# Two fused transformer blocks on one core: a third tile joins the block-interleaved opening after a norm, and the second sum moves behind it

## The chip, the cores and the metric

One core of one Trainium2 chip runs the whole program. The metric is the device time of one launch in microseconds (us); less is better.

## What is computed

A sequence of 512 tokens of width 1024 goes through a first block (an RWKV-7 mix and dilated attention, cross attention to a memory of 256 tokens, a squared-ReLU feed-forward) and then through a second block of two layers (a Fourier mix and a chunked retention, then a feed-forward with a width-3 convolution over tokens), with a normalisation ahead of each part. What matters here is the form that recurs at each part's border:

```
h = h + gate * (y @ w_last)                     # residual, [512 tokens, 1024]
n = h * rsqrt(mean(h*h, over 1024) + 1e-6) * g  # norm: one number per token
n = n * (1 + scale) + shift                     # second block only
z = n @ w_next                                  # the next stage's matmuls
```

The norm needs the sum over all 1024 features of a token before the first product of the next stage can start for that token.

## The kernel before, in words

Activations lie with the features on the partitions: 8 blocks of 128 features, each 512 tokens wide (`KT` = 8, `S` = 512). A matmul stage is a row of *tiles*: an output tile is 128 output features by 512 tokens in one of four PSUM banks, and sums 8 (or 6) blocks `k`. Each float32 product is made of three fp32r matmuls (L670 weights high x activation high, L671 weights high x activation low, L672 weights low x activation high).

Weights arrive in *units* of 128x1024 in a ring of four (`RING`): SyncE loads `w_raw`, ScalarE (ACT) casts it to `w_hi` (L1356), GpSimd (POOL) makes `w_lo` by four subtractions (L613), and TensorE (PE) waits for `w_low`. In the stages touched here a tile of 8 blocks has a unit of its own. ACT may cast a unit only when PE has ended the tile that used its slot four units earlier.

**Norms by token half.** At six places the norm is split into two halves of 256 tokens (`W2`). The names of the norms are `ffn` (closed by the stage `x_out`, followed by `up0`), `final` (closed by `down3`, followed by `fourier_in0`), `n2_0` and `n2_1` (closed by `out0`, `out1`, followed by `ff_in0_0`, `ff_in1_0`), `n1_1` (closed by `ff_out0_2`, followed by `fourier_in1`) and `out` (nothing follows). In the *closing* stage the last four tiles (`TAIL`) are made half by half. Then:

- VectorE (DVE) adds a tile half into the residual `H` (L1984 without a gate, L1985 with one), ACT squares it (L1416), DVE adds the squares up (L1938).
- PE sums over the partitions with four small products, `both_sums` (L706 for the running sum, L710 for the last square; at `final` a second pair L722, L726).
- DVE makes the statistic (L1919; four small operations at `final`), POOL raises it to -1/2 (L627), PE spreads it over the partitions into a bank (`spread_half`, L789).
- DVE multiplies block j of H by it into `tmp` (L2039), ACT makes the high part (L1376), DVE the low part (L1900, or L1898 at `ffn`). PE may use block j of that half once its low part is there.

The order of the DVE in `split_halves` is written by hand: blocks i = 0 to 7 are of the first token half, 8 to 15 of the second. Ahead of i = 1, 3, 5 it also takes the remaining tiles' second halves (`LATE_AT`), ahead of i = 6 it makes the statistic of the second half (`STAT_AT`), and there it waits for PE's sum of that half. The low part of block i-1 always follows the `tmp` of block i. The spread of the second half is waited for ahead of i = 8.

The *opening* of the next stage is `opening_halves` on PE: its first three tiles t0, t0+1, t0+2 are made half by half. The first half goes block by block over the first two tiles, and PE's sum of the second half stands behind block 2, its spread behind block 6. Then comes the whole first half of t0+2, then the second half of the first two tiles block by block, then the second half of t0+2. After the opening, the next tiles are made whole (512 tokens).

ACT's part in the closing is `closing` at L1421: squares and casts. `spare_slots(name)` says how many units of the next stage have a free slot before the last closing tile has ended: 1 for `n1_1` (its closing stage has tiles of 6 blocks, so the last units hold more than a tile), and 0 for all the others. POOL's program makes the low part of that spare unit ahead of the first half's L627 (`half_requests`), in the order in which the requests stand.

Of the kernel before, what the change touches and what calls it, by code (L numbers as in the profile page):

```python
# [25 lines left out]
KT = D // P  # L26
# [197 lines left out]
def build_program(nc, plan, ap, out):  # L224

    tiles, stages, conv, splits = plan.tiles, plan.stages, plan.conv, plan.splits
# [8 lines left out]
    for u in sorted(last_block):  # L235
        t, i = last_block[u]
# [7 lines left out]
    with ctx:  # L244
# [5 lines left out]
        def sem(name):  # L250
            if name not in sems:
                sems[name] = ctx.enter_context(nc.semaphore(name))
            return sems[name]
# [161 lines left out]
        def evacuated(eng, t):  # L415

            eng.wait_ge(sem(f"bank_free{bank_of(t)}"), tiles[t]["use"])
# [132 lines left out]
        def spare_slots(name):  # L550

            t0, t1 = stages[CLOSED[name]][0] + FULL, stages[CLOSED[name]][1] - 1
            return RING - 1 - tiles[t1]["blocks"][-1][0] + tiles[t0]["blocks"][0][0]
# [78 lines left out]
        def _(pe):  # L632
# [81 lines left out]
            def both_sums(norm, h):  # L714

                sum_half(norm, h)
                if norm == "final":
                    s = FULL + TAIL * h + TAIL - 1
                    chunks = range(TC // 2 * h, TC // 2 * (h + 1))
                    pe.wait_ge(sem("scaled_sq_used"), s)  # L720
                    for c in chunks:
                        nc.tensor.matmul(banks[5][:, TC + c:TC + c + 1], scaled_square_sum[:, c * P:(c + 1) * P],  # L722
                                         ones[:, 0:1], start=(c == chunks[0]), stop=False, skip_group_check=True)
                    pe.wait_ge(sem("scaled_sq_ready"), s + 1)
                    for c in chunks:
                        mm = nc.tensor.matmul(banks[5][:, TC + c:TC + c + 1], scaled_squares[:, s % 2, c * P:(c + 1) * P],  # L726
                                              ones[:, 0:1], start=False, stop=True, skip_group_check=True)
                    mm.then_inc(sem("scaled_sq_used"), 1)

            def spread_half(norm, h):  # L730

                if norm == "final":
                    pe.wait_ge(sem("both_inverses"), h + 1)
                spread(banks[7 if h else 4], W2, first=TC // 2 if norm == "final" else 0)
# [16 lines left out]
                for t in (t1 - 2, t1 - 1):  # L751
                    tile(t, splits[split][0], half=1, norm=norm)

            def opening_halves(name, split, norm):

                t0 = stages[name][0]
                for k in range(KT):
                    for t in (t0, t0 + 1):
                        tile(t, splits[split][0], only=k, half=0)
                    if k == 2:  # L760
                        both_sums(norm, 1)
                    if k == KT - 2:
                        spread_half(norm, 1)
                tile(t0 + 2, splits[split][0], half=0)
                for k in range(KT):
                    for t in (t0, t0 + 1):
                        tile(t, splits[split][0], only=k, half=1)
                tile(t0 + 2, splits[split][0], half=1)

            def spread_residual():  # L770

# [176 lines left out]
            t0 = stages["rkv1"][0]  # L948
# [134 lines left out]
            t0, t1 = stages["attn_out"]  # L1083
# [91 lines left out]
            for c, _ in enumerate(chunks_of(FF1)):  # L1175
                for name, split in ((f"up{c}", "n_ffn"), (f"down{c}", f"hidden{c}")):
                    t0, t1 = stages[name]
# [25 lines left out]
            for l in range(LAYERS):  # L1203
                t0 = stages[f"fourier_in{l}"][0]
# [13 lines left out]
                def fourier_tokens(j):  # L1218
# [16 lines left out]
                    mm.then_inc(sem("f_made"), 1)  # L1235

                opening_halves(f"fourier_in{l}", f"n1_{l}", f"n1_{l}" if l else "final")
                if l == 0:
                    spread_residual()
# [90 lines left out]
        def _(act):  # L1330
# [55 lines left out]
            def cast_opening(name, count):  # L1386

                if count:
                    cast_to(max(u for t in range(stages[name][0], stages[name][0] + count) for u, _, _ in tiles[t]["blocks"]))
# [31 lines left out]
            def closing(name, following=None):  # L1421

                t0 = stages[CLOSED[name]][0]
                for j in range(FULL):
                    follow(t0 + j)
                    evacuated(act, t0 + j)
                    square(name, j, H[:, j, :])
                    if name == "final":
                        scaled_square(j, j, slice(0, S))
                follow(t0 + FULL)  # L1430
                for j in range(FULL, KT):
                    square_half(name, j, 0)
                    cast_to(tiles[t0 + KT - 1]["blocks"][-1][0])
                if following:
                    cast_opening(following, spare_slots(name))
                square_half(name, FULL, 1)
                if following:
                    cast_opening(following, 1)
# [264 lines left out]
            t0, t1 = stages["mem_v"]  # L1703
# [32 lines left out]
            t0 = stages["x_out"][0]  # L1736
# [4 lines left out]
            for c, _ in enumerate(chunks_of(FF1)):  # L1741
                q = splits[f"hidden{c}"][0]
                t0, t1 = stages[f"up{c}"]
# [17 lines left out]
            for l in range(LAYERS):  # L1761
# [6 lines left out]
                t0 = stages[f"fourier_in{l}"][0]  # L1768
# [75 lines left out]
                for c, (a, n) in enumerate(chunks_of(FF2)):  # L1844
                    t0 = stages[f"ff_in{l}_{c}"][0]
# [13 lines left out]
                    t0 = stages[f"ff_out{l}_{c}"][0]  # L1859
# [872 lines left out]
```

## Time and profile before

| | |
|---|---|
| median of the 3 runs | 3442.48 us (3441.59 to 3443.18) |
| the profiled execution's own time | 3446.2 us |
| its span, first to last instruction | 3444.4 us |
| PE busy | 3358.8 us (98%) |
| DVE, ACT, POOL busy | 1573.0, 1124.5, 1567.3 us |
| mean granted TensorE clock | 0.994 of full |

PE is busy nearly all the time, so a change of order can only win or lose in the short stretches where it waits, and in the stretches where its granted clock is below 1. A busy PE in the table says little, as each matmul's recorded 0.28 us overlaps the next one, which starts 0.12 us later. The distance between two starts is the measure to use.

### The profile page before, as it was taken

To read this page: it belongs to the slowest core of one execution; us is meant where nothing else is said; L and a number is where in the kernel's file an instruction comes from. 1 tells how busy PE (TensorE), PEld (TensorE's weight loads), DVE (VectorE), ACT (ScalarE), POOL (GpSimd) and SP (SyncE) were. 2 spreads that over 40 slices of the span, in tenths; PEclk is the share of its full clock that TensorE was granted. 3 is DMA by queue.
4 is the path that set the end of the run, shared out by engine and by line. 5 is a ranking of instruction groups with operands and counts; after the bars stand their busy time and mean duration, and the time that the engine had idled before them with its cause. 6 is when DMAs were issued, how large, how long until landed. Compare 5 with 4: busy or idle time off the path is not lost.

```text
span 3444.4 us, 46412 instructions
## 1 busy us (share of the span) xinstructions
PE 3358.8 (98%) x17992; PEld 2821.8 (82%) x17992; DVE 1573.0 (46%) x2347; ACT 1124.5 (33%) x1780; POOL 1567.3 (46%) x1932
## 2 busy tenths in 40 slices
PE   7989999999999999999999999999999999999998
PEld 6768888888887888888887878888888787788887
DVE  2347766675232376666312214734551222255435
ACT  3333333333224332224322223423332222243323
POOL 4312111221456376764353345656534443556555
PEclk9999999999999999999999999999999999999999
DMA  4201000011333156672232223233222322223232
GB/s 151 68 25 39 25 25 25 25 48 36 125 95 120 62 208 238 239 255 80 74 105 78 67 85 98 86 98 105 87 71 86 97 73 79 86 86 106 91 98 92
DMA packets 91834, 321.70 MB, mean 93 GB/s; under 512 B 9952, under 2 KB 14176, under 8 KB 91360
## 3 DMA queue, kind: packets, MB, share of 16 engines
q1 hardware_dynamic: 83936, 299.93, 26.9%
q10 hardware_dynamic: 7680, 18.80, 1.6%
q8 instruction: 144, 2.36, 0.3%
q14 instruction: 74, 0.61, 0.1%
HBM read 314.76 MB, written 3.93 MB: 93 GB/s over the span
## 4 chain that ended last, share of the span: by engine, by line
PE 68%; POOL 13%; issue 12%; DVE 5%; DMA 1%; ACT 1%; POOLq 0%; DVEq 0%; SPq 0%; ACTq 0%
PE bank L670 16%; PE bank L672 15%; PE bank L671 15%; POOL w_lo L613 12%; PE bank L905 5%; PE bank L911 2%; PE bank L1277 1%; PE bank L663 1%; PE bank L665 1%; PE bank L664 1%; DMA w_raw<-in_weights 1%; PE bank L1214 1%; PE bank L1290 1%; DVE act L1900 1%; PE bank L846 1%
## 5 line engine op out<-in xcount | busy, mean ns | idle before, releaser
L613 POOL TENSOR_TENSOR w_lo<-w_raw,w_hi 128x256 fp32r<-128x256 f32 x1888 | 1520.8, 838 | 1248.4 <-ACT w_hi L1356 1248.2
L670 PE MATMUL bank<-act,w_hi 128*128 128x512 f32 (+1 forms) x3776 | 1440.5, 381 | 16.4 <-POOL w_lo L613 9.4
L672 PE MATMUL bank<-act,w_lo 128*128 128x512 f32 (+1 forms) x3776 | 1406.7, 373 | 0.0
L671 PE MATMUL bank<-act,w_hi 128*128 128x512 f32 (+1 forms) x3776 | 1406.1, 372 | 0.0
L670 PEld LDWEIGHTS bank<-act,w_hi 128*128 128x128 f32 x3776 | 716.3, 190 | 150.9 <-issue 31.0
L672 PEld LDWEIGHTS bank<-act,w_lo 128*128 128x128 f32 x3776 | 715.4, 189 | 123.6
L671 PEld LDWEIGHTS bank<-act,w_hi 128*128 128x128 f32 x3776 | 716.6, 190 | 120.1 <-issue 5.7
L1356 ACT CAST w_hi<-w_raw 128x1024 fp32r<-128x1024 f32 x472 | 489.3, 1046 | 393.1 <-PE bank L672 182.2
L627 POOL TENSOR_TENSOR stats<-stats,exponent 128x8 f32<-128x8 f32 (+2 forms) x39 | 46.9, 1204 | 627.8 <-DVE stats L1919 436.7
L1364 ACT ACTIVATE arena<-bank 128x512 f32<-128x512 f32 (+2 forms) x203 | 117.6, 585 | 511.5 <-PE bank L672 504.0
L905 PE MATMUL bank<-arena 128*128 128x128 f32 (+1 forms) x1920 | 247.1, 276 | 3.5 <-DVE arena L2269 2.5
L905 PEld LDWEIGHTS bank<-arena 128*128 128x128 f32 x1920 | 231.3, 192 | 16.3 <-issue 6.6
L1898 DVE TENSOR_TENSOR act<-tmp,act 128x512 fp32r<-128x512 f32 (+1 forms) x172 | 145.8, 848 | 84.5 <-ACT act L1376 78.2
L1376 ACT CAST act<-tmp 128x512 fp32r<-128x512 f32 (+1 forms) x172 | 100.2, 586 | 178.8 <-DVE tmp L2513 48.2
L1589 ACT ACTIVATE arena<-bank 128x512 f32<-128x512 f32 x144 | 85.1, 597 | 155.3 <-PE bank L911 155.0
L2583 DVE TENSOR_SCALAR arena<-arena,params 128x512 f32<-128x512 f32 x88 | 51.3, 583 | 178.1 <-ACT arena L1364 177.8
L2378 DVE TENSOR_TENSOR arena<-arena,bank 128x512 f32<-128x512 f32 x32 | 22.0, 687 | 235.9 <-PE bank L672 235.9
L2447 DVE SCALAR_TENSOR_TENSOR arena<-arena,small 128x1024 f32<-128x1024 f32 x84 | 122.0, 1453 | 3.0
L2056 DVE SCALAR_TENSOR_TENSOR arena<-bank,small,arena 128x512 f32<-128x512 f32 x48 | 36.0, 751 | 169.2 <-PE bank L672 169.0
L911 PE MATMUL bank<-table,arena 128*128 128x128 f32 x640 | 97.0, 276 | 13.1 <-DVE arena L2269 8.9
L663 PE MATMUL bank<-w_hi,act 128*128 128x256 f32 (+2 forms) x352 | 108.4, 308 | 1.3 <-POOL w_lo L613 1.3
L664 PE MATMUL bank<-w_lo,act 128*128 128x256 f32 (+2 forms) x352 | 106.7, 303 | 0.0
(251 smaller groups left out, 3054.7 us busy)
## 6 DMA issues: line engine op xcount, KB each, us to landing
w_raw<-in_weights SPq DMA_DIRECT2D x472, 512.0 KB, 3.5
arena<-in_ada SPq DMA_DIRECT2D x96, 512.0 KB, 4.4
arena<-in_strips ACTq DMA_DIRECT2D x8, 448.0 KB, 4.4
arena<-in_x ACTq DMA_DIRECT2D x4, 512.0 KB, 8.0
arena<-in_x ACTq DMA_DIRECT2D x1, 2048.0 KB, 8.0
y_scratch<-tmp ACTq DMA_DIRECT2D x7, 256.0 KB, 2.7
arena<-y_scratch ACTq DMA_DIRECT2D x1, 1792.0 KB, 9.1
arena<-in_dft ACTq DMA_DIRECT2D x2, 896.0 KB, 4.6
```

The source lines that it names most:

```text
L613: ins = nc.gpsimd.tensor_tensor(w_lo[:, k, cols], w_raw[:, k, cols], w_hi[:, k, cols].bitcast(F32), ALU.subtract)
L663: nc.tensor.matmul(o, xs[0], wh, start=first, stop=False)
L664: nc.tensor.matmul(o, xs[0], wl, start=False, stop=False)
L670: nc.tensor.matmul(o, wh, xh, start=first, stop=False)
L671: nc.tensor.matmul(o, wh, xl, start=False, stop=False)
L672: mm = nc.tensor.matmul(o, wl, xh, start=False, stop=last)
L905: mm = nc.tensor.matmul(b[:, w * i:w * (i + 1)], lhs[:, c, :], rhs(c), start=True, stop=True)
L911: mm = nc.tensor.transpose(b[:, P * i:P * (i + 1)], src[:, 4 * h + i, :], ident)
L1356: nc.scalar.copy(w_hi[:, k, :], w_raw[:, k, :]).then_inc(sem("w_high"), 1)
L1364: nc.scalar.activation(dst, banks[bank_of(t)][:, 0:n], func, scale=scale).then_inc(sem(f"bank_free{bank_of(t)}"), 1)
L1898: do(V_.tensor_tensor(o, x, h, ALU.subtract), "low_done")
L2447: do(V_.scalar_tensor_tensor(o, w, c_act[:, k:k + 1], o, ALU.mult, ALU.add), "ada_used")
```

## The change

Three things move; nothing is added to or taken out of any engine's work.

1. On PE, in `opening_halves`: in the first token half, tile t0+2 runs beside the first two from block 4 of these on, four blocks behind (`lag`), rather than behind them. In the second token half all three tiles go block by block.
2. On PE: the sum of the second half stands behind block 4 (and behind the third tile's block 0), no longer behind block 2. The spread stays behind block 6, but three blocks of the third tile now stand ahead of it.
3. On ACT, in `closing`: the spare unit of the next stage is cast after the first of the four half squares, no longer after the last. As `spare_slots` is 0 elsewhere, this moves one instruction, at `n1_1`.

```diff
-            def opening_halves(name, split, norm):
+            def opening_halves(name, split, norm, lag=4):
 
                 t0 = stages[name][0]
+                for k in range(KT + lag):
+                    if k < KT:
+                        for t in (t0, t0 + 1):
+                            tile(t, splits[split][0], only=k, half=0)
+                    if k >= lag:
+                        tile(t0 + 2, splits[split][0], only=k - lag, half=0)
+                    if k == 4:
+                        both_sums(norm, 1)
+                    if k == 6:
+                        spread_half(norm, 1)
                 for k in range(KT):
-                    for t in (t0, t0 + 1):
-                        tile(t, splits[split][0], only=k, half=0)
-                    if k == 2:
-                        both_sums(norm, 1)
-                    if k == KT - 2:
-                        spread_half(norm, 1)
-                tile(t0 + 2, splits[split][0], half=0)
-                for k in range(KT):
-                    for t in (t0, t0 + 1):
+                    for t in range(t0, t0 + 3):
                         tile(t, splits[split][0], only=k, half=1)
-                tile(t0 + 2, splits[split][0], half=1)
...
                 for j in range(FULL, KT):
                     square_half(name, j, 0)
                     cast_to(tiles[t0 + KT - 1]["blocks"][-1][0])
-                if following:
-                    cast_opening(following, spare_slots(name))
+                    if following:
+                        cast_opening(following, spare_slots(name))
                 square_half(name, FULL, 1)
```

How the instructions stand. PE at the opening of `ff_in0_0` (norm `n2_0`; its tiles t0, t0+1, t0+2 are in bank2, bank3, bank0), around the sum of the second half. Before, behind block 2 of t0+1:

```order
L672 MATMUL bank3<-act1,w_lo 128x256
L706 MATMUL bank5<-table,square_sum 128x1 x2
L710 MATMUL bank5<-table,squares 128x1 x2
L670 MATMUL bank2<-act1,w_hi 128x256
L671 MATMUL bank2<-act1,w_hi 128x256
```

With the change, behind block 4 of t0+1 and block 0 of the third tile (bank0):

```order
L672 MATMUL bank3<-act1,w_lo 128x256
L670 MATMUL bank0<-act1,w_hi 128x256
L671 MATMUL bank0<-act1,w_hi 128x256
L672 MATMUL bank0<-act1,w_lo 128x256
L706 MATMUL bank5<-table,square_sum 128x1 x2
L710 MATMUL bank5<-table,squares 128x1 x2
L670 MATMUL bank2<-act1,w_hi 128x256
```

The row behind L710 was block 3 of t0; it is now block 5 of t0. The other openings read alike.

ACT in the closing of `n1_1`. Before, the cast of the spare unit is the second L1356 here:

```order
L1356 CAST w_hi<-w_raw 128x1024
L1416 ACTIVATE squares<-arena 128x256 x4
L1356 CAST w_hi<-w_raw 128x1024
L1416 ACTIVATE squares<-arena 128x256
L1762 DMA arena<-in_dft 128x1792
```

With the change (the same lines, one number up):

```order
L1357 CAST w_hi<-w_raw 128x1024
L1417 ACTIVATE squares<-arena 128x256
L1357 CAST w_hi<-w_raw 128x1024
L1417 ACTIVATE squares<-arena 128x256 x4
L1763 DMA arena<-in_dft 128x1792
```

The cast passed three of the half squares. DVE, POOL and SyncE keep their order.

## Rows read from the trace of the kernel before

**Rows 1.** The page, part 1: busy time of each engine.
```profile
PE 3358.8 (98%) x17992; PEld 2821.8 (82%) x17992; DVE 1573.0 (46%) x2347; ACT 1124.5 (33%) x1780; POOL 1567.3 (46%) x1932
```

**Rows 2.** Waits of PE, 1190 to 3100 us: total us, times, longest.
```profile
PE bank L706 <- DVE square_sum L1938: 3.9, 4, 1.4
PE bank L710 <- ACT squares L1416: 2.2, 4, 1.2
```

**Rows 3.** Timeline of PE, n2_0: start, us, what, [idle before <-releaser].
```profile
2148.57 0.28 PE L672 MATMUL bank<-act,w_lo 128*128 128x256 f32 x1
2149.72 0.61 PE L706 MATMUL bank<-table,square_sum 128*128 128x1 f32 x4 [0.88 <-DVE square_sum L1938]
2150.69 0.61 PE L710 MATMUL bank<-table,squares 128*128 128x1 f32 x4 [0.36 <-ACT squares L1416]
```

**Rows 4.** Timeline of DVE, n2_0: low parts 3, 4; statistic; low part 5.
```profile
2148.32 0.48 DVE L1900 SCALAR_TENSOR_TENSOR act<-tmp,small,act 128x256 fp32r<-128x256 f32 x1
...
2150.22 0.48 DVE L1900 SCALAR_TENSOR_TENSOR act<-tmp,small,act 128x256 fp32r<-128x256 f32 x1
...
2151.39 0.16 DVE L1919 TENSOR_SCALAR stats<-bank 128x2 f32<-128x2 f32 x1 [0.17 <-PE bank L710]
...
2152.11 0.48 DVE L1900 SCALAR_TENSOR_TENSOR act<-tmp,small,act 128x256 fp32r<-128x256 f32 x1
```

**Rows 5.** Timelines, norm ffn: PE's sum without a wait, DVE's statistic.
```profile
1212.85 0.50 PE L706 MATMUL bank<-table,square_sum 128*128 128x1 f32 x4
...
1213.74 0.37 PE L670 MATMUL bank<-act,w_hi 128*128 128x256 f32 x1
...
1213.97 0.16 DVE L1919 TENSOR_SCALAR stats<-bank 128x2 f32<-128x2 f32 x1 [0.23 <-PE bank L710]
```

**Rows 6.** PE in windows: from:to us, busy (count), granted clock, DMA share, GB/s.
```profile
1211.00:1216.00 5.00, 5.00 (x43) 1.00 0.92 334
...
2152.80:2155.80 3.00, 3.00 (x16) 0.50 0.00 0
```

**Rows 7.** Timeline of PE, norm final: the waits ahead of the two sums.
```profile
1596.41 0.61 PE L706 MATMUL bank<-table,square_sum 128*128 128x1 f32 x4 [0.78 <-DVE square_sum L1938]
1598.17 0.61 PE L710 MATMUL bank<-table,squares 128*128 128x1 f32 x4 [1.16 <-ACT squares L1416]
```

**Rows 8.** Timelines at n2_0: PE's first whole tile, ACT's cast of t0+5.
```profile
2168.69 0.40 PE L670 MATMUL bank<-act,w_hi 128*128 128x512 f32 x1
2168.92 0.40 PE L671 MATMUL bank<-act,w_hi 128*128 128x512 f32 x1
...
2172.95 1.05 ACT L1356 CAST w_hi<-w_raw 128x1024 fp32r<-128x1024 f32 x1 [1.34 <-DVE arena L2586]
```

**Rows 9.** Page, part 5: the group of POOL's subtractions.
```profile
L613 POOL TENSOR_TENSOR w_lo<-w_raw,w_hi 128x256 fp32r<-128x256 f32 x1888 | 1520.8, 838 | 1248.4 <-ACT w_hi L1356 1248.2
```

**Rows 10.** Timelines at n1_1: ACT takes t0, DVE's fold, PE's use.
```profile
2536.06 1.08 ACT L1364 ACTIVATE arena<-bank 128x512 f32<-128x512 f32 x2
...
2538.92 0.71 DVE L2504 TENSOR_TENSOR arena<-arena 128x128 f32<-128x128 f32 x1
...
2540.85 1.46 PE L1214 MATMUL bank<-arena 128*128 128x256 f32 x6
```

**Rows 11.** Timelines behind norm final: DVE's fold, PE's use of it.
```profile
1621.08 0.29 DVE L2504 TENSOR_TENSOR arena<-arena 128x128 f32<-128x128 f32 x1
...
1621.51 0.67 PE L1214 MATMUL bank<-arena 128*128 128x256 f32 x2 [0.16 <-DVE arena L2504]
```

**Rows 12.** Timelines, n1_1, first half: ACT's cast, DVE's statistic, POOL, PE's spread.
```profile
2504.97 1.03 ACT L1356 CAST w_hi<-w_raw 128x1024 fp32r<-128x1024 f32 x1
...
2507.06 0.16 DVE L1919 TENSOR_SCALAR stats<-bank 128x2 f32<-128x2 f32 x1 [2.45 <-PE bank L710]
...
2508.83 0.70 POOL L627 TENSOR_TENSOR stats<-stats,exponent 128x2 f32<-128x2 f32 x1
...
2509.59 0.71 PE L789 MATMUL bank<-table,stats 128*128 128x128 f32 x4 [1.08 <-POOL stats L627]
```

## The prediction, made before the changed kernel ran

> **What bounds the kernel now.** I read the page's busy times first: PE is busy for 98% of the span [rows 1], so what this change of order can win or lose lies where PE waits or runs at a lower clock. Next the waits of PE over the stretch that holds the five openings: 3.9 us ahead of L706, 2.2 us ahead of L710 [rows 2], and once 1.1 us ahead of L789 [rows 12]. All lie in the norms. Then the timelines. At `n2_0`, block 2 of t0+1 has its last start at 2148.57, then PE sits until 2149.72 for DVE's running sum, and again ahead of L710 for ACT's last square [rows 3]. At `final` the same two waits are 0.78 and 1.16 us [rows 7]. At `ffn` there is neither [rows 5]. Last the granted clock in windows: behind the `n2_0` waits it is 0.50, the 1.2 GHz level, and PE starts 16 matmuls in 3.00 us; at clock 1.00 there are 43 in 5.00 us [rows 6]. The same lower stretch follows the waits at `final`, `n1_1` and `n2_1`, with 15 or 16 matmuls in 3.00 us each; at `ffn` there is none. What PE did before each fall was to wait and to make one-column sums.
>
> From these rows: a matmul of 256 tokens starts 0.12 us after the last (5.00 / 43), so a block of one tile is 0.36 us and a block of three tiles 1.08 us. At the lower clock the step is 0.19 to 0.21 us, so a lower stretch costs about 16 x 0.09 = 1.5 us where PE has work all through it. A sum that waits for nothing is 0.89 us (1212.85 to 1213.74), and the statistic starts 1.12 us after the sum does [rows 5].
>
> **The sum behind block 4, at n2_0.** Up to block 2 nothing changes: PE is through at 2148.57 + 0.12 = 2148.69. Block 3 needs low part 3, ready at 2148.80, so it runs 2148.84 to 2149.56. Block 4 needs low part 4, which DVE ends at 2150.22 + 0.48 = 2150.70 [rows 4]. So PE waits here for 1.2 us, about what the sum waited. The wait at the sum is gone but is not saved. Blocks 4, 4 and the third tile's 0 end at 2151.90, the sum at 2152.79, and the statistic starts at 2151.90 + 1.12 = 2153.02, where it was 2151.39.
>
> Here a new wait arises. DVE stands at its statistic, and queued behind it are tmp 6 and then low part 5, in this order. Low part 5 ends 2152.59 - 2151.39 = 1.20 us after the statistic starts [rows 4], now at 2154.22. PE's next instruction is block 5 of t0, which needs it. Before, blocks 3 and 4 of two tiles (4 x 0.36 = 1.44 us) stood between the sum and block 5, and covered this chain. Now nothing does: **PE waits 2154.26 - 2152.79 = 1.4 us.** The third tile's block 1 would fit there, but it stands behind block 5.
>
> From there: blocks 5 and 6 with the third tile's (2 x 1.08, and 0.08 for a first matmul after a wait) end at 2156.50, the spread takes 0.36, seven blocks 2.52, and the 24 blocks of the second half 8.64 and about 0.1. The opening ends at 2168.1. It ended at 2168.69 [rows 8], 1.3 us of that by the lower clock, so 2167.4 at a full one. The order alone is worth +0.7 us: two waits of 2.6 us for 1.6 us before, less about 0.3 us at blocks of the second half, which three tiles per block (1.08 us) give DVE time to make. The same steps with the rows of the other openings give +0.8 at `ffn` (no wait before, 1.4 us after), +0.6 at `final` (a wait of 2.0 us for low part 4, 2.2 us for low part 5, as there two pairs of sums and four statistics stand in the chain), +0.6 at `n1_1` and `n2_1`. Sum: **+3.2 us**.
>
> **The clock.** The sum and its waits at `n2_0` left PE without wide matmuls for 2.5 us (2148.69 to 2151.16), and the clock fell. Now 1.2 + 0.9 + 1.4 = 3.5 us are without them, with 1.16 us of work between. I expect the fall at the four places again, about 0.2 us dearer each at three, since more work stands behind; at `final`, where 5.9 us are without work, a longer one (+1.0 us); and a new one at `ffn` (+1.4), where 0.9 + 1.4 us are. Sum: **+2.8 us**. Both ends: 0 if the clock falls as before, and minus 4 x 1.5 = -6 if it no longer falls at all; +6 if it stays low for a second stretch at four places.
>
> **What follows the opening.** Tile t0 ended about 3.2 us before the opening's end (the eight blocks of t0+2, and one of t0+1); now it ends 0.72 us before it. ACT casts the unit of t0+4 on t0's end and only then takes t0 out of its bank, so this chain comes 2.6 us later against PE. (a) At `n1_1` DVE's fold of t0 ended at 2539.63, 3.57 us after ACT's take began, and PE used it at 2540.85 [rows 10]: 1.2 us of cover. It will be 2.6 us later, less the cover: **+1.6 us** with what the wait takes to end. (b) Behind `final`, the fold waits for a residual spread that stays in place, but POOL's subtractions of t0+4 now lie on it. A fold operation of 128 columns takes 0.29 us without POOL [rows 11] and 0.71 us beside it [rows 10]; the wait there is already on PE's path: **+0.9 us**. (c) At `n2_0` and `n2_1` the cast of t0+5 hangs on DVE's second convolution, 4.3 us after the opening's end [rows 8]. At 6.9, and with 1.1 for the cast and 3.4 for POOL's part (4 x 838 ns [rows 9]), the unit is ready 11.4 us after. PE needs it two tiles after, at 11.0 (24 matmuls of 512 tokens at 0.23 us each [rows 8]): **+1.0 us** for both. At `ffn` 0.1 to 1 us of cover remains. The three sum to 3.5 us; bounds 0 (DVE and ACT catch up) and 7 (each late by the whole 2.6).
>
> The SBUF — State Buffer page of the Trainium skill ("SBUF: two separate sides") says that a DVE operation with two SBUF inputs and a GpSimd operation that reads SBUF exclude each other for a whole instruction. By that, each of the four fold operations could lose up to a whole subtraction of POOL, and (b) would be near 3 us by the page's rule. The trace agrees in kind, 0.29 to 0.71 us [rows 10, 11], and the sum uses the rows.
>
> **The cast.** At `n1_1` ACT cast the spare unit at 2504.97, POOL's low part of it ran until 2508.83, and only then came L627, though the statistic had been there since 2507.22; PE waited until 2509.59 [rows 12]. Cast some 6 us sooner, POOL is free, L627 ends near 2508.0, and PE, ready at 2508.35, does not wait: **-1.2 us**. The cast holds up nothing: the next half square comes 1 us after it would end. Its bounds are -1.3 and 0 (if the slot is not free then, but the tile that used it ends before it).
>
> **Sum:** 3.2 + 2.8 + 3.5 - 1.2 = +8.3 us. Against the profiled execution's 3446.2 us that is 3454.5; the median of the runs lies 3.7 us lower, 3442.5, so I predict **3450.8 us**. A measurement of this kernel can tell about 0.2%, 6.9 us, from no change.
>
> **The rivals.** *The new wait, with clock and followers as forecast*: 3450.8, chance 0.55. *The order alone*: the clock falls as before and ACT and DVE catch up, so 3.2 - 1.2 = +2 us, to +6 with half of the followers: 3444 to 3449, chance 0.24. For it speaks that both followers have some cover, which the rows show only to 1 us. *Clock low twice*: a second lower stretch at three or four places, and units late for PE: +13 to +16 us, 3455 to 3459, chance 0.14. *Faster*: DVE's low part 5 is not the limit. PE would lose its waits of 3.9 + 2.2 us [rows 2], four lower stretches of 1.5 us and the 1.2 us of the cast: -13 us, 3429. It decides at block 5: low part 5 must be ready when the sum ends. Its chain hangs on that very sum, by 1.45 us at least, so only a mistake in the order I read would give it; chance 0.04. *Only the cast works*, all the rest even: -1 us, 3441, chance 0.03.
>
> **The range** takes in 3444 to 3458: it leaves out the two cases at the fast side, and the far end of the slow one. The chances: faster by over 0.2% is the fourth case, 0.04. Slower by over 0.2% is above 3449.4: three quarters of the first case, whose middle lies 1.4 us above that bound, and all of the third, 0.41 + 0.14 = 0.55. The rest, 0.41, lies within.
>
> **What would show it.** In the profile of the changed kernel: at each of the five openings a wait of PE at block 5 (L670 for DVE's L1900 or L1898) of 1.4 us, 2.2 at `final`, and one at block 4 at four of them; waits of L706 and L710 gone; statistic 1.6 us later against the closing stage; a lower clock also behind `ffn`; a wait of about 1.6 us for L2504 at `fourier_in1`; no wait at L789 (L790 there) at `n1_1`. It is wrong if low part 5 is there before the sum ends, or if the lower stretches go.

## The result, and the profile after

The changed kernel takes 3458.04 us (median of 4 runs, 3456.72 to 3459.87). The kernel before, run beside it, takes 3442.69 us (4 runs, 3441.59 to 3443.18). The ratio is 1.004, with a 95% interval of 1.0028 to 1.0052: slower, by 15.4 us, where +8.3 us was forecast. A second measurement, with 5 runs against 15, gave 3460.15 against 3444.03 us: 1.0047 (1.0034 to 1.0061); one of the 15 was a slow run of 6827 us, which the ratio leaves out. The profiled execution of the changed kernel took 3456.72 us (span 3454.9, mean granted clock 0.994), that of the second measurement 3459.49 us (span 3457.7, clock 0.993).

The page of the changed kernel, part 1, busy time of each engine:

```profile
PE 3356.0 (97%) x17992; PEld 2818.5 (82%) x17992; DVE 1579.8 (46%) x2347; ACT 1124.5 (33%) x1780; POOL 1573.7 (46%) x1932
```

The instructions are as many as before [rows 1]; DVE and POOL are each busy for 6 to 7 us more. The time is lost where PE waits and where its clock is low. Its waits from 1190 to 3110 us (total us, times, longest):

```profile
PE bank L670 <- DVE act L1901: 11.2, 9, 2.1
PE bank L670 <- POOL w_lo L613: 9.2, 9, 3.5
...
PE bank L670 <- DVE act L1899: 1.3, 1, 1.3
PE bank L1215 <- issue: 1.2, 1, 1.2
PE bank L1215 <- DVE arena L2505: 0.9, 1, 0.9
```

The two rows of before, 3.9 us at L706 and 2.2 us at L710 [rows 2], are gone. In their place stand 12.5 us at L670 for DVE's low parts. At `n2_0`, PE's timeline of the changed kernel reads:

```profile
2156.77 0.38 PE L670 MATMUL bank<-act,w_hi 128*128 128x256 f32 x1 [0.94 <-DVE act L1901]
2157.95 0.50 PE L706 MATMUL bank<-table,square_sum 128*128 128x1 f32 x4
2158.31 0.58 PE L710 MATMUL bank<-table,squares 128*128 128x1 f32 x4
2160.24 0.43 PE L670 MATMUL bank<-act,w_hi 128*128 128x256 f32 x1 [1.35 <-DVE act L1901]
```

The first wait is at block 4, the two sums run without one, and the last wait is at block 5. Against before [rows 3], two waits of 1.24 us in all have become two of 2.29 us. The chain of waits of the changed kernel shows what the second is made of (start, us, what):

```profile
2158.45 0.46 PE bank L710 x4
2158.91 0.03 DVEq L1916
...
2158.99 0.17 DVE stats L1920
2159.18 0.49 DVE tmp L2040
...
2159.70 0.50 DVE act L1901
...
2160.24 0.43 PE bank L670
```

So it is as forecast: the end of the sum releases DVE's statistic, DVE then makes `tmp` 6 and only behind it low part 5, and PE has nothing else to do. The low part is there 1.21 us after the statistic starts, as before (1.20 us) [rows 4]. The statistic itself starts 13.39 us after the spread of the first half (2158.99 - 2145.60), where it was 11.79 us: 1.6 us later, as forecast.

**Where the clock fell.** Windows of PE (from:to us, busy and count, granted clock, DMA share, GB/s), each around one place (`down0` is the stage behind `up0`; its first tile comes some 30 us behind the opening at `ffn`). First the changed kernel: `down0`, `final`, `n2_0`, `n1_1`, `n2_1`:

```profile
1255.00:1270.00 15.00, 11.45 (x41) 0.77 0.64 216
1595.00:1615.00 20.00, 15.80 (x112) 0.83 0.32 102
2148.00:2168.00 20.00, 17.70 (x133) 0.91 0.34 105
2510.00:2540.00 30.00, 27.09 (x202) 0.89 0.36 119
3065.00:3095.00 30.00, 27.71 (x229) 1.00 0.23 71
```

The changed kernel in the second measurement, `ffn` and then the same places from `down0` on:

```profile
1210.00:1225.00 15.00, 13.71 (x103) 0.89 0.43 171
1255.00:1270.00 15.00, 11.46 (x51) 1.00 0.71 244
1595.00:1615.00 20.00, 15.80 (x98) 0.74 0.28 81
2148.00:2168.00 20.00, 17.70 (x133) 0.91 0.33 105
2510.00:2540.00 30.00, 27.12 (x201) 0.89 0.39 119
3065.00:3095.00 30.00, 27.71 (x209) 0.89 0.22 71
```

The kernel before, `n2_0` and `n2_1` (at `final` it reads 0.91, at `n1_1` 0.94):

```profile
2148.00:2168.00 20.00, 18.70 (x141) 0.91 0.21 74
...
3065.00:3095.00 30.00, 28.71 (x196) 0.94 0.24 72
```

A window of 20 us at 0.91 holds 3.6 us at half clock (0.09 x 2 x 20). Counted so over the five openings, PE had 14.4 us at the 1.2 GHz level before, 17.0 us in the changed kernel's first profile and 30.5 us in its second, and the first has 6.9 us more at `down0`. PE's waits for DVE were the same in both profiles (12.5 and 12.4 us), and the one at `down0` too (3.5 us); where the clock fell differs.

**Against the stretches.** The same matmul was found in two traces and its two starts subtracted; what the difference gains over a stretch is what the stretch cost. "Opening" is up to the first whole tile, "behind" is the next tile or two (for `ffn`, up to `down0`'s first tile). In us, against the trace before, which is one and the same execution for all columns and lay 3.7 us above its median, so that a column reads some us lower than the medians do:

| stretch | change | change, second | sum back | old second half | statistic later | filled | filled, ffn as before | take first |
|---|---|---|---|---|---|---|---|---|
| up to `ffn` | -1.5 | -2.1 | -2.6 | -1.7 | -0.6 | -1.2 | -0.7 | -1.7 |
| opening `ffn` | +0.9 | +2.4 | -0.5 | +3.3 | -0.2 | -0.1 | 0 | 0 |
| behind `ffn` | +4.4 | +1.9 | +3.5 | 0 | +3.5 | +3.2 | 0 | 0 |
| opening `final` | +1.7 | +3.3 | -0.9 | +4.5 | +0.7 | -1.3 | -0.6 | -0.6 |
| behind `final` | +0.8 | +0.8 | +0.8 | 0 | +0.8 | +0.8 | +0.8 | +1.0 |
| opening `n2_0` | +0.9 | +1.0 | -1.9 | +2.4 | -1.6 | -2.6 | -2.6 | -2.6 |
| behind `n2_0` | +1.2 | +1.2 | +1.2 | 0 | +1.2 | +1.2 | +1.2 | +0.3 |
| closing of `n1_1` | -1.4 | -1.3 | -1.3 | -1.4 | -1.3 | -1.3 | -1.4 | -1.3 |
| opening `n1_1` | +1.9 | +2.1 | -0.3 | +3.1 | -0.5 | -2.6 | -2.5 | -2.6 |
| behind `n1_1` | +1.5 | +1.5 | +1.5 | 0 | +1.5 | +1.5 | +1.5 | 0 |
| opening `n2_1` | -0.5 | +2.0 | -1.8 | +3.1 | -1.5 | -2.5 | -2.6 | -2.5 |
| behind `n2_1` | +0.9 | +0.9 | +0.9 | 0 | +0.9 | +0.9 | +0.9 | +0.3 |
| the whole span | +10.5 | +13.3 | -1.7 | +13.5 | +2.4 | -4.1 | -6.0 | -9.7 |

The columns behind the first two are experiments, in the order of the sections below. Stretches that are not listed differ by 0.5 us or less in all. Ahead of `ffn` the change moves nothing; that row goes with the clock from 1000 to 1190 us, which was 0.97 of full in the trace before, 0.99 in the change's first profile and 1.00 in its second.

**Behind `ffn`** is the largest single row, and the forecast had nothing there. PE's first tile of `down0`, in the trace of before and in that of the change:

```profile
1259.55 0.47 PE L670 MATMUL bank<-act,w_hi 128*128 128x512 f32 x1 [1.66 <-POOL w_lo L613]
```

```profile
1260.85 0.76 PE L670 MATMUL bank<-act,w_hi 128*128 128x512 f32 x1 [3.55 <-POOL w_lo L613]
```

POOL's timeline of the 32 us ahead of it, before:

```profile
1227.96 8.31 POOL L613 TENSOR_TENSOR w_lo<-w_raw,w_hi 128x256 fp32r<-128x256 f32 x8 [7.86 <-ACT w_hi L1356]
1237.62 4.70 POOL L613 TENSOR_TENSOR w_lo<-w_raw,w_hi 128x256 fp32r<-128x256 f32 x4 [1.35 <-ACT w_hi L1356]
1243.06 9.92 POOL L613 TENSOR_TENSOR w_lo<-w_raw,w_hi 128x256 fp32r<-128x256 f32 x8 [0.74 <-ACT w_hi L1356]
1253.94 5.46 POOL L613 TENSOR_TENSOR w_lo<-w_raw,w_hi 128x256 fp32r<-128x256 f32 x4 [0.96 <-ACT w_hi L1356]
```

and with the change:

```profile
1229.90 36.83 POOL L613 TENSOR_TENSOR w_lo<-w_raw,w_hi 128x256 fp32r<-128x256 f32 x30 [9.50 <-ACT w_hi L1357]
```

POOL starts the unit of t0+4 late, because that unit's cast waits for tile t0, which now ends late: 0.66 us behind the end of the opening (1229.90 against 1229.24), where it was 1.86 us ahead of it (1227.96 against 1229.82), so 2.5 us later against PE. Before, POOL had three gaps (1.35 + 0.74 + 0.96 = 3.05 us), and PE waited even then. The three are gone now, which would take the lateness in, but the 24 subtractions ahead of `down0`'s first tile take 30.8 us in place of 28.4. In this stretch a subtraction takes 0.73 us where no DVE operation is under way at its start, and about 1.18 or 1.72 us where one is; five of the 24 were of the short kind before, one is with the change. So 1.9 of the 2.5 us reach PE.

**The fold and the cast** came as forecast. Behind `final` and at `n1_1` the changed kernel's PE shows a wait in front of L1215:

```profile
1627.52 0.67 PE L1215 MATMUL bank<-arena 128*128 128x256 f32 x2 [0.95 <-DVE arena L2505]
...
2550.87 1.32 PE L1215 MATMUL bank<-arena 128*128 128x256 f32 x5 [1.22 <-issue]
```

It was 0.16 us and nothing [rows 10, 11]. The second one is put down to "issue", but it ends with DVE's fold: its last operation ran from 2550.07 for 0.70 us. ACT's order decides it too, as an experiment below shows. And the spread of the first half at `n1_1`, one line up from L789, waits for nothing, where PE waited 1.08 us [rows 12]; POOL's subtractions end at 2512.13, 3 us ahead of the statistic:

```profile
2507.31 4.82 POOL L613 TENSOR_TENSOR w_lo<-w_raw,w_hi 128x256 fp32r<-128x256 f32 x6
2515.39 0.69 POOL L627 TENSOR_TENSOR stats<-stats,exponent 128x2 f32<-128x2 f32 x1 [3.27 <-DVE stats L1920]
2516.43 0.60 PE L790 MATMUL bank<-table,stats 128*128 128x128 f32 x4
```

### The profile page after: what moved, and what is told of

It reads as the page before. It is cut to its first block, busy times and chain, and to the rows that moved or that the text cites. A ratio compares the mean times of both kernels' runs of the same rounds, so it can differ in the third digit from the quotient of the medians.

```text
span 3454.9 us, 46412 instructions
## 1 busy us (share of the span) xinstructions
PE 3356.0 (97%) x17992; PEld 2818.5 (82%) x17992; DVE 1579.8 (46%) x2347; ACT 1124.5 (33%) x1780; POOL 1573.7 (46%) x1932
## 3 DMA queue, kind: packets, MB, share of 16 engines
q8 instruction: 144, 2.36, 0.3%
## 4 chain that ended last, share of the span: by engine, by line
PE 71%; POOL 11%; issue 11%; DVE 5%; ACT 1%; DMA 1%; POOLq 0%; DVEq 0%; SPq 0%; ACTq 0%
PE bank L670 17%; PE bank L672 16%; PE bank L671 16%; POOL w_lo L613 11%; PE bank L906 5%; PE bank L912 2%; PE bank L1278 1%; PE bank L663 1%; PE bank L665 1%; PE bank L664 1%; PE bank L1215 1%; PE bank L1291 1%; PE bank L847 1%; PE bank L790 1%; PE bank L876 1%
## 5 line engine op out<-in xcount | busy, mean ns | idle before, releaser
L670 PE MATMUL bank<-act,w_hi 128*128 128x512 f32 (+1 forms) x3776 | 1441.2, 382 | 32.9 <-POOL w_lo L613 13.6
L670 PEld LDWEIGHTS bank<-act,w_hi 128*128 128x128 f32 x3776 | 716.5, 190 | 169.1 <-issue 36.1
L663 PE MATMUL bank<-w_hi,act 128*128 128x256 f32 (+2 forms) x352 | 108.0, 307 | 2.9 <-POOL w_lo L613 2.9
L665 PE MATMUL bank<-w_hi,act 128*128 128x256 f32 (+2 forms) x352 | 106.5, 302 | 0.0
```

Of the source, the lines that this page charges most:

```text
L663: nc.tensor.matmul(o, xs[0], wh, start=first, stop=False)
L665: mm = nc.tensor.matmul(o, xs[1], wh, start=False, stop=last)
L670: nc.tensor.matmul(o, wh, xh, start=first, stop=False)
```

## The experiments

### The cast alone

The kernel before, with the third part of the change only:

```diff
                     cast_to(tiles[t0 + KT - 1]["blocks"][-1][0])
-                if following:
-                    cast_opening(following, spare_slots(name))
+                    if following:
+                        cast_opening(following, spare_slots(name))
```

> The kernel before with the cast of n1_1's spare unit after the first half square, and nothing else. The theory (POOL is late for the statistic of n1_1's first half only because it still makes the spare unit's low part): PE's wait of 1.1 us at L789 goes, nothing else moves, 1.2 us less than before, 3441.5. The rival (the earlier subtractions hold up DVE's adds in the closing stage, which then end later): no gain, 3442.7, with the sum of the first half later than before against the closing tiles.

Measured: 3442.49 us against 3443.34, ratio 0.9999 (0.999 to 1.0008). The wait in front of the spread is gone and the closing of `n1_1` is 1.35 us shorter, in this trace as in all the others with the cast. A gain of 0.04% does not show in the medians, which cannot tell 3441.5 from the rival's 3442.7; the trace does.

This trace tells something else too. It differs from the one before in a single instruction's place, and yet its span is 5.1 us shorter: besides the cast's 1.35 us, 1.9 us ahead of `ffn`, 0.9 at the opening of `n2_0` and 0.8 at that of `n2_1`. At the last two its clock did not fall:

```profile
2148.00:2168.00 20.00, 19.50 (x147) 1.00 0.18 55
...
3065.00:3095.00 30.00, 29.49 (x191) 1.00 0.24 71
```

At `final` and `n1_1` it fell as before. So a fall at a given opening is no fixed thing, and the profiled execution of before, 3.7 us above its median, was one with more of them. The kernel before shows the same with nothing moved: its executions in the second measurement run from 3441.26 us at a mean granted clock of 0.997 to 3449.31 us at 0.992. The forecast took its four falls for the rule.

### The second sum back behind block 2

The change, with the third tile where it puts it, but the sum in its old place:

```diff
-                    if k == 4:
+                    if k == 2:
                         both_sums(norm, 1)
```

> The change with the sum of the second half behind block 2 again (the third tile still four blocks behind, the second half by three tiles, the early cast). First theory (the sum behind block 4 makes the wait at block 5): the waits of PE for low part 5 (1.3 us at four openings, 2.1 us at final) go, the old waits at L706 and L710 come back (about 6 us in all), and what follows the openings stays as late as in the change: 6 us less than the change, 3452. Rival (the place of the sum does not matter, the order of the second half does): as the change within 1 us, 3457 to 3459.

Measured: 3445.72 us against 3443.34, ratio 1.0009 (1.0000 to 1.0018): 12 us below the change, twice what was expected. The waits in front of L706 and L710 are back (3.9 and 2.2 us), the followers are what they are with the change, and the openings cost 10.3 us less. So the sum's place is the costly part. In this trace it is dearer than the waits it makes (12.5 us in place of 6.1), since at `n2_0` and `n2_1` the clock did not fall (1.00 in both windows) and at `final` and `n1_1` it fell for half as long.

### The second half in its old order

The change, with t0 and t0+1 first and then t0+2 in the second token half:

```diff
-                    for t in range(t0, t0 + 3):
+                    for t in (t0, t0 + 1):
                         tile(t, splits[split][0], only=k, half=1)
+                tile(t0 + 2, splits[split][0], half=1)
```

> The change with its second half as before: two tiles block by block, then the third. First theory (what follows an opening is late because t0 ends only 0.7 us before the opening's end): the long wait for w_lo at down0's first tile falls from 3.5 us back to about 1.8 us, the fold at fourier_in1 is in time, and the waits at block 5 stay. The openings end 1.2 us later each (low part 14 sets the end), so the whole is about 2 us less than the change, 3456. Rival (the order of the second half is all that costs): as the kernel before within 2 us, 3441 to 3445.

Measured: 3457.69 us against 3443.34, ratio 1.0041 (1.0028 to 1.0054), the same as the change, where 3456 was expected. All the followers are gone (0 in all five rows of the table), which shows that the late end of t0, which the three-tile second half brings, caused every one of them. The openings pay it back. This trace has the clock falls of the change's second profile, and its openings cost 16.4 us where those cost 10.8. PE's timeline at `n2_0` shows why; here are the first matmuls of three successive blocks of t0 in the second half:

```profile
2168.72 0.39 PE L670 MATMUL bank<-act,w_hi 128*128 128x256 f32 x1
...
2169.76 0.39 PE L670 MATMUL bank<-act,w_hi 128*128 128x256 f32 x1
...
2170.80 0.39 PE L670 MATMUL bank<-act,w_hi 128*128 128x256 f32 x1
```

Two tiles per block are 0.72 us of work, and they come 1.04 us apart: DVE makes a low part in 1.04 us, and PE loses 0.3 us at each block, in pieces too short for the table of waits. Three tiles per block take 1.08 us and lose nothing. At `n2_0` the old order costs 1.4 us here (2.36 against 0.95). The kernel before lost only some 0.3 us in this way, as the forecast had it, since there the whole first half of t0+2 stood ahead of the second half and gave DVE a lead.

### The statistic one block later on DVE

The change, with DVE's statistic of the second half ahead of i = 7. Low part 5 then no longer stands behind it:

```diff
-        LATE_AT, STAT_AT, CAST_AT = (1, 3, 5), 6, (0, 2, KT - 1)
+        LATE_AT, STAT_AT, CAST_AT = (1, 3, 5), 7, (0, 2, KT - 1)
```

> The change with one number altered: DVE makes the second half's statistic ahead of its block 7, no longer ahead of block 6. PE's order is that of the change. First theory (the wait at block 5 is the chain statistic, tmp 6, low part 5 behind the sum): low part 5 is ready before the sum ends, the waits of 1.3 us at block 5 fall to nothing, one of about 0.3 us appears at block 6 (1 us at final), and the lower clock is rarer; about 1 us less at each opening, 6 us less than the change in all, 3451 to 3453. Rival (PE waits at block 5 since ACT and DVE are simply that slow per block): the waits keep their length, 3457.

Measured: 3447.10 us against 3442.88, ratio 1.0011 (1.0003 to 1.0020): 11 us below the change, nearly twice what was expected. PE at `n2_0`, ahead of the sum and at block 5:

```profile
2155.81 0.50 PE L706 MATMUL bank<-table,square_sum 128*128 128x1 f32 x4
...
2158.10 0.38 PE L670 MATMUL bank<-act,w_hi 128*128 128x256 f32 x1 [0.17 <-DVE act L1901]
```

The block-5 wait has shrunk from 1.35 to 0.17 us, by one instruction moved on an engine that is busy for 46% of the span. The clock at `n2_0` and `n2_1` stayed at 1.00. This is the cleanest proof that the wait is DVE's order behind the late sum: nothing on PE moved. The wait at block 4 is as in the change (0.93 us), and the kernel stays slower than the one before.

### The waits filled from the third tile

Blocks of t0+2 are at hand, so PE can do them where it would wait. The first half as a row of steps, where a digit is a block of t0 and t0+1, a letter a block of t0+2 (a is 0), S the sum and P the spread:

```diff
-                for k in range(KT + lag):
...
+                for step in ("0123abcS4def56g7Ph" if norm == "final" else "0123abcS4de5Pf67gh"):
```

The second half is as in the change, and the cast too.

> A first half in another order: blocks 0 to 3 of the two tiles, the third tile's 0 to 2, the sum, block 4, the third tile's 3 and 4, block 5 and so on (at final one block more between sum and block 5), with the second half and the cast of the change. First theory (what costs is that PE has nothing in its order between the sum and low part 5): no wait of PE over 0.3 us from block 3 to block 7 except at final (1 us for ACT's last square), no lower clock behind four of the five openings, openings that end 3 us sooner than before at four places and even at ffn; the followers stay as late as in the change (8 us in all). About 6.5 us less than before, 3436. Rival (the clock falls wherever the one-column sums stand, whatever is around them): the lower stretches stay at four places, 3441 to 3443.

Measured: 3443.41 us against 3443.34, ratio 0.9999 (0.999 to 1.0008). The openings gain: they are 9.1 us shorter than before. But the followers are there, with 7.6 us, 3.2 of them behind `ffn`. Expected was 3436, with 8 us of followers counted in. What fell short is the gain at the openings (3 us at four places expected, 2.5 to 2.6 measured at three and 1.3 at `final`) and the base: the span is 4.1 us shorter than that of the trace before, the median the same, as the execution in that trace was a long one.

With the old second half besides:

```diff
-                    for t in range(t0, t0 + 3):
+                    for t in (t0, t0 + 1):
                         tile(t, splits[split][0], only=k, half=1)
+                tile(t0 + 2, splits[split][0], half=1)
```

> The filled first half with the second half of the kernel before (two tiles block by block, then the third) and the early cast. First theory (DVE makes a block per 1.04 us in the second half and PE takes 0.72 us for two tiles, so the opening ends 4.3 us after low part 14, and the followers are in time): openings end about 1.9 us later than in the filled order, no wait for w_lo over 1.9 us at down0, none over 0.3 us at the folds; within 1 us of the filled order, 3442.5. Rival (the three-tile second half wins nothing): 8 us less than the filled order, 3435.

Measured: 3443.01 us against 3442.88, ratio 0.9999 (0.999 to 1.0008). No followers now, and the openings are back to -0.4 us in all. Both forms end where the kernel before does: the three-tile second half is worth 8.7 us at the openings here and costs 7.6 behind them.

### The opening at ffn left alone

There no wait could be won [rows 5], and the follower is dearest:

```diff
+                order = {"final": "0123abcS4def56g7Ph", "ffn": "012S3456P7abcdefgh"}
...
+                    for t in range(t0, t0 + (2 if norm == "ffn" else 3)):
...
+                if norm == "ffn":
+                    tile(t0 + 2, splits[split][0], half=1)
```

> The filled order of the last experiment, with norm ffn's opening wholly as in the kernel before. First theory (the late wait at down0's first tile comes from ffn's opening alone: t0 ends 1.9 us later there, and POOL's subtractions then run without a gap up to down0): the wait for w_lo at down0 is 1.8 us again, no lower clock follows it, and 3 to 4.4 us are won over the filled order, all ahead of 1262 us: 3438 to 3440. Rival (that wait has another cause, such as how the transfers fall): it stays at 3.5 us and the time stays at 3443.4.

Measured: 3439.73 us against 3442.88, ratio 0.9986 (0.9977 to 0.9995). Its repeat:

> The filled order with ffn as before once more, on the same chip as e8: as it was, 3 us less than before.

Measured: 3439.63 against 3443.44 us, ratio 0.9988 (0.9979 to 0.9997). The interval stays below 1 in both: faster, by 3 to 4 us. Windows of the first of the two at `n2_0`, `n1_1` and `n2_1`:

```profile
2148.00:2168.00 20.00, 19.75 (x153) 1.00 0.21 68
2510.00:2540.00 30.00, 27.93 (x202) 1.00 0.21 71
3065.00:3095.00 30.00, 29.13 (x189) 1.00 0.23 64
```

### ACT takes t0 before it casts for t0+4

What is left are the followers behind four openings, 4.4 us. ACT hangs both on t0's end: first the cast of t0+4's unit, then the taking of t0 out of its bank, on which DVE's fold or convolution waits. Exchanged, at the four openings other than `ffn` (the second piece stands behind the activation that takes a tile out of its bank):

```diff
-                cast_opening(following, 5)
+                if norm == "ffn":
+                    cast_opening(following, 5)
+                else:
+                    pending.append(following)
...
+                if pending:
+                    cast_opening(pending.pop(), 5)
```

> The filled order with ffn as before, and ACT takes t0 out of its bank before it casts the unit of t0+4, at the four openings other than ffn's. Theory for what follows an opening (ACT's cast of 1.05 us stands ahead of the take, and DVE's fold or convolution behind it): the fold at fourier_in1 is about 1 us sooner, so PE's wait there falls from 1.5 us to under 0.5, the waits behind n2_0 and n2_1 (1.2 and 0.9 us) fall to 0.2 or less, the one behind final stays at 0.8, as it hangs on the residual spread; 3 us less than the filled order with ffn as before, 3437. Rival (POOL's subtractions beside DVE set these waits, not ACT's order): they stay as they are or grow, since the cast is later, 3440 or more.

Measured: 3436.49 us against 3443.44, ratio 0.9977 (0.9968 to 0.9986). Its timeline at `n1_1`, ACT and then PE:

```profile
2530.12 0.60 ACT L1369 ACTIVATE arena<-bank 128x512 f32<-128x512 f32 x1 [2.04 <-PE bank L672]
2530.61 1.04 ACT L1361 CAST w_hi<-w_raw 128x1024 fp32r<-128x1024 f32 x1
...
2533.34 1.89 PE L1218 MATMUL bank<-arena 128*128 128x256 f32 x8
```

The take runs first and PE finds the fold done: the wait of 1.2 us is gone. The followers at `n2_0`, `n1_1` and `n2_1` fall from 3.6 to 0.6 us. The one behind `final` stays (+1.0): PE waits there for the first fold however ACT is ordered.

> The filled order with ffn as before and the early take, once more, beside the change on the same chip: 7 us under before, 0.9968 to 0.9986 again, and some 20 us under the change.

Measured: 3437.57 against 3444.03 us, ratio 0.9978 (0.9969 to 0.9987). This version beats the kernel before by 6.5 to 7 us, the changed one by about 22.

### The change once more

> The change itself once more, beside the kernel before on one chip. The profiled executions differ by 10.5 us and the medians by 15.4. If the rest is where the granted clock falls from one execution to the next (the profiled one fell in three of the five openings and stayed up at ffn and n2_1), this profile shows it fall at ffn or n2_1 too, with 1 to 2 us more in the stretch concerned and the same waits to 0.1 us. If it is something else, a stretch outside the openings and what follows them differs from the first profile by over 1 us with the clock at full. Time 12 to 15 us over before.

Measured: 3460.15 us (3459.49 to 3460.75) against 3444.03, as told at the top. Its waits for DVE are those of the first profile (11.1 us in place of 11.2 for L1901), its clock is not: it fell at `ffn` and at `n2_1` too, and these openings cost 1.5 and 2.5 us more. The time is 16.1 us over before, where 12 to 15 were expected.

## Why the prediction was right, and where it was short

The sign and the mechanism held; the size, +8.3 us forecast and +15.4 measured, did not. The 3458.04 us lie at the very end of the range, and among the times of the third rival, "Clock low twice" (3455 to 3459, chance 0.14), not near the 3450.8 of the first. The sum has slips too, which change little: its terms for the order add up to 3.3 us and not 3.2, those for the clock to 3.0 and not 2.8, and 2154.26 - 2152.79 is 1.5 us, not 1.4.

**The order, +3.2: right.** Predicted was a wait at block 5 of 1.4 us, and of 2.2 at `final`. Measured were 1.29 (`ffn`), 1.35 (`n2_0`) and 2.1, for the reason given. Block 4 waited too, 0.94 of the forecast 1.2 us; the rest came one block sooner. The openings' rows sum to +4.9 and +10.8. Taken off these the time at the lower clock at half its length (2.6 us more than before in the first profile, 16.1 in the second: 1.3 and 8.0, an estimate from above, as PE did not have work all through it), 3.6 and 2.8 us are left for the order. Moving DVE's statistic alone took 11 us back, so this wait and the clock that hangs on it are most of the change.

**The clock, +2.8: the mechanism right, the size short.** One fall at each place was forecast, a new one at `ffn` and a longer one at `final`. The second profile shows just these, but also lower stretches twice as long at `n1_1` and `n2_1` (0.89 of 30 us, where before had 0.94): up to +8 us in place of 2.8, while the first has +1.3. In the first profile `ffn` and `n2_1` were spared, and `down0` had a long one. The failed step is "about 0.2 us dearer each at three". What the forecast gave 0.14, a second lower stretch at three or four places (3455 to 3459), is what happened at two or three of them. That the second profile is no exception is seen from all the executions of its measurement: their mean granted clock is 0.9928 on average against 0.9953 of the kernel before, or some 17 us more at the lower level (2 x 0.0025 x 3459), worth at most half of that. Where the clock falls differs between executions, and the two profiles lie 2.8 us apart.

**What follows, +3.5: short by 5.3 us in the first profile, by 2.8 in the second.** (a) `n1_1`: 1.6 forecast, 1.5 measured. (b) `final`: 0.9 forecast, 0.8 measured. (c) `n2_0` and `n2_1`: 1.0 together forecast, 2.1 measured, of which the exchange of take and cast took back 1.5. The failed step is "At `ffn` 0.1 to 1 us of cover remains". There was none, as PE waited there for POOL already, 1.66 us. That wait is 1.9 us longer with the change (second profile: +1.9 for the row), and where the clock fell behind it the row is 3.2 to 4.4. The row stood in the trace, but at `down0`, some 30 us behind the opening, and I had looked only at the next tiles.

DVE's fold behind `final` had been weighed against a rule of the Trainium skill. Its two 256-column operations took 0.79 and 0.84 us beside POOL where they had taken 0.42 and 0.43, the two of 128 columns 0.29 us as before: 0.8 us in all. By the rule of the Trainium skill (SBUF — State Buffer, "SBUF: two separate sides"), up to a whole subtraction of POOL for each of four operations, it would have been near 3, by estimate. The trace decides for the row's price: the two operations that ran beside POOL are slower by 0.4 us each, less than a whole subtraction (0.84 us on average [rows 9]), and POOL was through at 1626.43, ahead of the other two (1626.75 and 1627.08). It does not show by itself whether the two engines exclude each other.

**The cast, -1.2: right**, -1.35 measured in all the traces.

**The base.** The sum was made against an execution 3.7 us above its median, and the same 3.7 us were taken off the result. The profiled execution of the change was 1.3 us below its own median. That makes up the gap between the profiles' +10.5 and the medians' +15.4. The trace with the cast alone shows where an execution of the kernel before can be shorter: 1.9 us ahead of the first opening and 1.7 us at `n2_0` and `n2_1`, where its clock stayed up. An execution that has no fall there has more to lose to the change than the forecast's base showed.

**The rivals.** "The order alone" (3444 to 3449) falls: the followers came, and the clock was low for longer. "Clock low twice" came in part, at two places in one profile and three in the other. "Faster" falls: low part 5 was not there when the sum ended. "Only the cast works" falls with the time.

**Open.** Why the clock falls at one place in one execution and not in the next, with the same waits, was not settled, so how the 15 us divide between the waits and the clock is known only by estimate. Nor was it tried to end the wait for the first fold behind `final`, or to give POOL at `down0` less to do.

## What to carry to other kernels

When a reduction is moved behind more work to hide its wait, look at the in-order queue of the engine that consumes it: what stands behind the consumer there becomes late too, and here PE needed it next; the cure was to move the consumer, or to put ready work at that point. When several tiles end together in place of one after another, follow what hangs on the first one's end through all engines and as far as the next place where PE already waits, since there is no cover there. And take the base of a sum from more than one execution where the clock can fall.

## What was not expected of the hardware

The granted clock at one place differs between executions of nearly the same instructions: 0.91 of 20 us at `n2_0` in the trace before, 1.00 with one cast moved. And at two openings where PE waited and made one-column sums for longer, the lower stretch was longer: at `n1_1` 3.6 us at the 1.2 GHz level before (0.94 of 30 us) and 6.6 us with the change (0.89), at `final` 3.6 us before and 10.4 us in one profile of the change (0.74 of 20 us). At `n2_0` it was not: 3.6 us before and in both profiles of the change, though the waits had grown from 1.24 to 2.29 us. Behind the wait at `down0`, which holds no sums, it was at the lower level for 6.9 us in one profile and not at all in the other, after 3.5 us of waiting in both. A microsecond of waits cost more than a microsecond: with the statistic one block later, PE's waits for DVE's low parts fell from 12.5 to 5.4 us, and the kernel's time by 11.

Between 1227 and 1262 us POOL's subtraction of 128x256 took 0.73 us where no DVE operation was under way at its start and 1.18 or 1.72 us in nearly all other cases. So POOL without a gap was not POOL at its own speed: of 3.05 us of gaps that closed, 2.4 us went into longer subtractions.
